# Heads' norm by square root and reciprocal, and the first sided operands ahead of a split, in a two-layer decoder step

## The reference

```
f = lb + (1.0 - lb) * jax.nn.sigmoid(fx.astype(jnp.float32))
o, S = hgrn2_scan(heads(jax.nn.silu(q.astype(jnp.float32))), heads(jnp.log(f)), heads(1.0 - f),
                  heads(ix), S0.astype(jnp.float32))
o = o.transpose(0, 2, 1, 3)
o = o * lax.rsqrt(jnp.mean(o * o, axis=-1, keepdims=True) + EPS)
o = o * hg_norm.astype(jnp.float32).reshape(HG_HEADS, HG_DV)
o = o.reshape(B, L, HG_WIDTH) * jax.nn.silu(g.astype(jnp.float32))
yp, new_buf = multiscale_pool(u, buf, start_pos, w_pool, pool_scale)
y = jnp.concatenate([o.astype(h.dtype), yp], axis=-1) @ w_o
```

## Time and profile before

| | before |
|---|---|
| timed runs, median | 888.22 us (886.88 to 888.23) |
| the profiled execution's own time | 886.84 us |
| its span, first to last instruction | 884.7 us |
| TensorE matmuls busy | 863.3 us, 98% of the span |
| VectorE busy | 686.4 us, 78% |
| ScalarE busy | 571.8 us, 65% |
| GpSimd busy | 173.3 us, 20% |
| granted TensorE clock, mean | 0.998 |

### The profile page before, as it was taken

One profiled execution on the slowest core, in us unless ns is written; L12 is line 12 of the kernel. 1 busy time (PEld: TensorE's weight loads), 2 busy tenths in 40 slices (PEclk: granted clock), 3 DMA queues, 4 the chain that ended last, 5 costly groups with the idle time before them and its releaser, 6 DMA issues.

```text
span 884.7 us, 14868 instructions
## 1 busy us (share of the span) xinstructions
PE 863.3 (98%) x5743; PEld 798.5 (90%) x5743; DVE 686.4 (78%) x814; ACT 571.8 (65%) x691; POOL 173.3 (20%) x151
## 2 busy tenths in 40 slices
PE   6999999999999999999999999999999999999996
PEld 6999899999999999999989888888888888888886
DVE  5886587777765548865796889989898989898964
ACT  6744666544543447546847778697878778787842
POOL 4332075555421122322610000000000000000001
PEclk9999999999999999999999999999999999999999
DMA  8833247555678526424374799999999999898911
GB/s 300 296 135 96 73 153 280 191 176 180 219 290 281 192 96 194 141 96 169 131 269 152 288 371 397 352 372 372 350 393 333 412 317 422 314 408 308 406 68 50
DMA packets 52406, 222.05 MB, mean 251 GB/s; under 512 B 6208, under 2 KB 6336, under 8 KB 51694
## 3 DMA queue, kind: packets, MB, share of 16 engines
q1 hardware_dynamic: 50670, 209.61, 64.9%
q0 software_dynamic: 960, 9.50, 2.8%
q10 hardware_dynamic: 720, 2.18, 0.6%
HBM read 214.25 MB, written 7.47 MB: 251 GB/s over the span
## 4 chain that ended last, share of the span: by engine, by line
PE 94%; DVE 2%; ACT 2%; issue 1%; DMA 1%; DVEq 0%; ACTq 0%
PE bank L1733 42%; PE bank L1427 12%; PE bank L1428 12%; PE bank L1429 12%; PE bank L1456 3%; PE bank L1705 2%; PE bank L1789 2%; PE bank L1575 2%; PE bank L1512 2%; PE bank L1742 1%; DVE sb_w_lo L953 1%; ACT sb_w_hi L555 1%; DMA sb_raw<-in_in_units_dram 1%; PE bank L1536 0%; PE bank L1567 0%
## 5 line engine op out<-in xcount | busy, mean ns | idle before, releaser
L953 DVE TENSOR_TENSOR sb_w_lo<-sb_raw,sb_w_hi 128x1024 fp32r<-128x1024 f32 (+1 forms) x116 | 169.5, 1462 | 65.1 <-ACT sb_w_hi L555 63.9
L555 ACT ACTIVATE sb_w_hi<-sb_raw 128x1024 fp32r<-128x1024 f32 (+1 forms) x116 | 127.1, 1102 | 122.4 <-PE bank L1429 119.7
L1427 PE MATMUL bank<-at_act_hi,sb_w_hi 128*128 128x264 f32 x672 | 194.3, 289 | 8.1 <-DVE sb_w_lo L953 8.1
L1428 PE MATMUL bank<-at_act_lo,sb_w_hi 128*128 128x264 f32 x672 | 191.7, 285 | 0.0
L1429 PE MATMUL bank<-at_act_hi,sb_w_lo 128*128 128x264 f32 x672 | 191.7, 285 | 0.0
L1733 PE MATMUL bank<-sb_w_hi,at_packed 128*128 128x512 f32 (+1 forms) x768 | 191.0, 378 | 0.0
L1000 DVE TENSOR_TENSOR sb_w_lo<-at_raw_e,sb_w_hi 128x1408 fp32r<-128x1408 f32 (+1 forms) x112 | 159.1, 1446 | 26.6 <-ACT sb_w_hi L623 25.4
L1000 DVE TENSOR_TENSOR sb_w_lo<-sb_raw,sb_w_hi 128x1408 fp32r<-128x1408 f32 (+1 forms) x104 | 150.2, 1479 | 18.9 <-ACT sb_w_hi L623 18.9
L623 ACT ACTIVATE sb_w_hi<-at_raw_e 128x1408 fp32r<-128x1408 f32 (+1 forms) x112 | 139.3, 1244 | 36.8 <-PE bank L1733 36.5
L1733 PEld LDWEIGHTS bank<-sb_w_hi,at_packed 128*128 128x128 f32 x768 | 139.8, 188 | 22.2
L623 ACT ACTIVATE sb_w_hi<-sb_raw 128x1408 fp32r<-128x1408 f32 (+1 forms) x104 | 130.5, 1262 | 35.6 <-PE bank L1733 34.7
(11 more groups left out here) (261 smaller groups left out, 1360.5 us busy)
## 6 DMA issues: line engine op xcount, KB each, us to landing
sb_raw<-in_moe_w_up_dram SPq DMA_DIRECT2D x36, 704.0 KB, 7.0
at_raw_e<-in_moe_w_down_dram SPq DMA_DIRECT2D x49, 512.0 KB, 6.2
at_raw_e<-in_moe_w_gate_dram SPq DMA_DIRECT2D x35, 704.0 KB, 8.7
sb_raw<-in_up_units_dram SPq DMA_DIRECT2D x44, 512.0 KB, 3.3
sb_raw<-in_moe_w_gate_dram SPq DMA_DIRECT2D x29, 704.0 KB, 8.2
sb_raw<-in_in_units_dram SPq DMA_DIRECT2D x39, 512.0 KB, 3.6
sb_raw<-in_moe_w_down_dram SPq DMA_DIRECT2D x39, 512.0 KB, 5.0
at_raw_e<-in_moe_w_up_dram SPq DMA_DIRECT2D x28, 704.0 KB, 6.2
```

What stands on the lines that cost most here:

```text
L555: act.activation(w_hi[s][:, 0:kts, :], raw[s][:, 0:kts, :], ACT.Copy).then_inc(hi_done, 1)
L953: dve.tensor_tensor(w_lo[s][:, 0:kts, :], raw[s][:, 0:kts, :], w_hi[s][:, 0:kts, :].bitcast(f32), ALU.subtract).then_inc(lo_done, 1)
L1427: pe.matmul(out[:, 0:T], w_hi[s][:, k, :], hi[:, c, :], start=(c == 0), stop=False)
L1428: pe.matmul(out[:, 0:T], w_hi[s][:, k, :], lo[:, c, :], start=False, stop=False)
```

## The change

Two edits, both in the mixer and so done twice, once in each layer.

The heads' norm: ScalarE takes Sqrt of the mean plus eps where it took Ln, with the table for Sqrt preloaded at L681 in the place of that for Ln. The three Exp go, and with them the table load in front of them. VectorE takes the reciprocals in place, in three instructions behind the last `scale_heads` (L1097) and ahead of `scale_head`. Each waits for its Sqrt.

The first sided operands: `side(0)` moves from the start of step (2, 2) to the end of step (2, 1), right behind the two sample products and so ahead of a split.

```diff
-                        act.preload_act_table(ACT.Ln)
+                        act.preload_act_table(ACT.Sqrt)
...
-                    act.activation(hg_rstd[:, :, tok], bank[n][:, cols].rearrange("p (h t) -> p h t", h=HEADS), ACT.Ln, scale=1.0 / 128,
+                    act.activation(hg_rstd[:, :, tok], bank[n][:, cols].rearrange("p (h t) -> p h t", h=HEADS), ACT.Sqrt, scale=1.0 / 128,
                                    bias=eps[:, :]).then_inc(hgo_rooted, 1)
-                for k, (_, _, tok) in enumerate(HG_SUMS):
-                    act.wait_ge(hgo_rooted, 3 * L + k + 1)
-                    act.activation(hg_rstd[:, :, tok], hg_rstd[:, :, tok], ACT.Exp, scale=-0.5).then_inc(hgo_rstd, 1)
...
-                    if 0 <= m < 8:
+                    if 0 < m < 8:
                         side(m)
...
                         dve.tensor_tensor(sample_kq[:, :, :], keys[:, :, SEQ:T], proj[:, 0, :, SEQ:T], ALU.mult).then_inc(kq_done, 1)
+                        side(0)
...
+                for k, (_, _, tok) in enumerate(HG_SUMS):
+                    dve.wait_ge(hgo_rooted, 3 * L + k + 1)
+                    dve.reciprocal(hg_rstd[:, :, tok], hg_rstd[:, :, tok]).then_inc(hgo_rstd, 1)
                 dve.wait_ge(hgo_rstd, 3 * (L + 1))
```

## The result

The changed kernel takes 890.98 us (median of six runs, 890.25 to 891.69), the kernel before 887.93 beside it: a ratio of 1.0041, with a 95% interval from 1.0031 to 1.005. It is slower by 3.05 us, and the forecast was 2.9. The profiled execution took 890.96 us around a span of 888.8; that of before took 886.84 around 884.7. So the two traces lie 4.1 apart, 1.1 more than the medians, and the difference matters: the runs of the kernel before fall in two groups, one from 886.7 to 887.6 us and one from 888.2 to 889.8, and the profile of before belongs to the first.

What follows compares the result with a forecast made beforehand. TensorE was taken to bound the kernel (94% of the chain that ended last), so gains lay in its waits. The norm's 3.84 us less the sided edit's 0.95 made 2.9 more: 891.1 us on the median, range 884.5 to 894.5.

Steps and rivals of the forecast that it cites:

- The norm: Heads' norm, both layers: VectorE's reciprocals outweigh the removed Exp and load; scale_head starts 1.92 us later per layer, 3.84 in two.
- the first reading: Norm's reciprocals: all that is not fixed cost is columns, 6.3 ns each, so 3.38 us for 512 columns.
- The prediction's 155: Norm's reciprocals: the fixed part taken as 155 ns, from small tensor_tensor rows, with columns priced on top.
- the 19 ns: Reciprocal of 3 columns: 174 less the base of 155, divided by 3 to give 6.3 ns a column.
- The sided edit in layer 0: First sided operands: the pair ends 1.56 us earlier, of which 0.95 is kept; bounds -0.4 to 1.56.
- The new wait: TensorE, layer 0, ahead of the scores after the first sided ones: a wait of about 0.6 us not there before.
- the second pair: Layer 0, operands of TensorE's next scores: ready at 52.27 before, only 0.35 us earlier, at 51.92, after the edit.
- VectorE's idle 0.32: Layer 0, first sided operands: VectorE gains the 0.32 us it idled before the split, as the pair fills it.
- The up to 1.0 us for turns at the norm: Layer 1's norm: GpSimd's five products lie over the first reciprocal; taking turns would cost up to 1.0 us.
- Rival 1: Norm: a short reciprocal, 0.70 us for 512 columns, removes TensorE's 0.93 wait in both layers; 885.4 us, chance 0.33.
- Rival 2: Norm: a longer reciprocal, 8.3 ns a column, makes scale_head 4.02 us later in each layer; 895.3 us, chance 0.15.
- Rival 3: Both edits cancel: GpSimd's turn eats the sided gain, reciprocal costs near 4.5 ns a column; 888.2 us, chance 0.05.

Runs made afterwards that it cites:

- another kernel: The changed kernel with twenty more unread transposes filling TensorE's wait at the norm in layer 1 alone: 890.27 us, ratio 1.0029.

## Why the prediction was right, step by step

**The norm: right in mechanism, a little too dear.** The choice of the first reading, that all of a reciprocal that isn't fixed is columns, carried the forecast, and between 32 and 512 columns it holds: 6.31 ns a column measured, 6.3 taken. What was wrong was the fixed part, 155 ns taken from the tensor_tensor, 92 measured. With that the way to the 6.3 falls too: the line through the two sizes gives 111 ns at 3 columns and 117 at 4, where the earlier trace rows have 174 and 178, and over the prediction's 155 a column would cost 6.2 ns at 512 columns and 4.3 at 32. So the 19 ns that were divided by 3 were not the price of three columns. That a column costs several ns was argued and is right; that the quotient was 6.3 is luck, and what the smallest reciprocals spend their time on stays open. Measured, 512 columns took 3.32 in place of 3.38 and 32 took 0.29 in place of 0.36, and each layer lost 1.72 where the sum has 1.92: 3.43 in two layers, not 3.84. Run with a cheap instruction in the reciprocals' place, the loss turned into a gain, so this price is shown to be the cause. The Trainium skill, VectorE: DVE Perf Modes, section First, the fixed hardware budget, gives a repeat count of 8, and by the estimate from it, at that page's 0.96 GHz, a column would be 8.3 ns. The measurement is 6.31.

**The sided edit in layer 0: right in mechanism, too small.** The split went first, as said, GpSimd waited, and the wait fell to 0.43 (0.4 said). The new wait ahead of the next scores was 0.23, not 0.6, so 1.1 to 1.2 was kept in place of 0.95. The mis-sized term is the second pair. It was to come 0.35 earlier than the 52.27 of the earlier trace rows, and it ended at 51.50, 0.77 earlier; less the 0.14 ahead of the edit, 0.63. VectorE's idle 0.32 went as said, and the split in front of the pair, which starts beside the end of GpSimd's difference, took 1.35 in place of 1.57: it now lies beside 0.27 us of that difference (48.94 to 49.21), before beside 0.49 (49.49 to 49.98).

**Layer 1 and GpSimd.** The edit gave nothing to speak of there, as said (the marks move by 0.1 between the layers). The up to 1.0 us for turns at the norm did not come: 6.78 in both layers.

**What was not in the sum: the clock.** In or behind a wait of TensorE its granted clock can fall to 0.50 for some us, which cost 1.3 to 2.4 us each time. In the changed kernel's two profiles it did so behind layer 1's norm, in one of the five profiles of the kernel before behind the wait of 1.98. The prediction took neither into account. By the traces alone the sum of the measured terms is 3.43 - 1.22 = 2.2 us, and the rest of the 4.1 is about 1.3 and 0.7 of clock. The forecast set 2.9 on a median that lies 1.4 above the trace it was made from, because many runs of the kernel before lie in the second group. So its terms were 0.7 too high and its base 1.4, and together these stood in for the 2.0 of clock that it left out. The loss and its mechanism were forecast; that the time came within 0.1 us is luck.

**The rivals.** Rival 1's working holds for a short instruction. At the router's first product the run with the cheap one is 1.85 us ahead of the sided edit alone (427.39 and 429.24), where the rival counts 2 x 0.93 = 1.86, but not in equal parts: 1.46 comes from layer 0 (first root of layer 1 at 410.69 and 412.13, that of layer 0 at 102.22 and 102.20), where the wait vanishes, and 0.4 from layer 1, where 0.52 of it is left. Its profiled execution lies 2.7 under that of before (884.15 and 886.84), where the rival says 2.8; that the median of 884.09 is under the 885.4 that the prediction gave is again the base. Rival 2's 8.3 ns are refuted by the 6.31. Rival 3's first half, that GpSimd's turn eats the sided gain, is refuted by the split's 1.22.

**Left open.** What decides behind which wait the clock falls, and when it does not: waits of 2.66 (layer 0 of the changed kernel) and of 1.28 passed without it in a profile, those of 0.93 did so in every one that was read, that of 1.98 in four of five profiles of the kernel before, and the one of 2.63 in layer 0 of another kernel brought the longest stretch.

## What to carry to other kernels

Before moving work from an engine with a table load to one with a costlier instruction, price the instruction per column near the size that it will have, since the rows of 3 and 4 columns could not say what 512 would cost. And ask whether its first input could simply come earlier: the load was hidden, with its three Exp, by moving three small sums in TensorE's program order. And measure two edits apart even where their sum is known; here one gained, one lost, and the pair looked like a small loss.

## What the runs showed of the hardware

A wait of TensorE can cost more than its length, in two ways. A listed wait of 0.93 gave back 1.36: the listed wait starts at the end that the profile models for the matmul before, which the next one overlaps by 0.25 where it does not wait, and the head blocks behind it were 0.19 shorter. And the granted clock can fall to 0.50 in or behind it, though not each time: 1.3 us with a wait of 2.63, 1.6 with one of 1.97, 2.4 with another of 2.63. Filling the waits with unused transposes took 1.3 us off the changed kernel (890.71 and 889.40).

A reciprocal of 512 columns (3.32 us) is not slowed by GpSimd's products beside it; a tensor_scalar over the same tile in the same place is: three took 4.66 us in layer 1 and under 1 in layer 0. The Trainium skill, SBUF — State Buffer, section SBUF: two separate sides, says that VectorE and GpSimd share a port pair, that VectorE takes it for an operation in a two-port mode, or for one with two inputs from that memory where GpSimd's operation reads it too, and that whichever starts first holds it for the whole instruction. The split behind the sided pair agrees (1.22 us, with GpSimd's difference at 2.81 in place of 1.89). That the tensor_scalar ran in such a mode and the reciprocal not would fit 0.43 us and 3.32 us for 512 columns, but no run here shows the mode itself. Nor does one show why the tensor_scalar of 4.23 us ended behind the last of GpSimd's five products and did not come in between two of them.
